# Token arrays split by chunk parity, and each level's transposed factor taken from the evicted factor one level later

## The chip, the core and the metric

One core of a Trainium2 chip runs the whole program. The metric is the device time of one execution in microseconds. The engines are TensorE (PE), VectorE (DVE), ScalarE (ACT), GpSimd (POOL) and SyncE (SP), which issues the DMAs. Each engine works through a queue of its own in program order, and they meet at semaphores.

## What is computed

A two-layer encoder over two sequences of 256 tokens, 1024 features: layer 0 mixes tokens with a bidirectional RWKV-7 recurrence (16 heads of 64), layer 1 with grouped-query attention, and each is followed by a gated MLP. The change lies in the recurrence, once per direction and head:

```python
def step(S, inp):
    r_t, w_t, k_t, v_t, a_t, b_t = inp
    sa = jnp.einsum('bhij,bhj->bhi', S, a_t)
    S = S * w_t[:, :, None, :] + sa[..., None] * b_t[:, :, None, :] + v_t[..., None] * k_t[:, :, None, :]
    return S, jnp.einsum('bhij,bhj->bhi', S, r_t)
y = (_wkv_scan(r4, dec4[0], kd4[0], v4, -kk, kk * a4[0], reverse=False)
     + _wkv_scan(r4, dec4[1], kd4[1], v4, -kk, kk * a4[1], reverse=True))
```

All of it is float32.

## The kernel before

The recurrence is done in chunks of C = 64 tokens. 512 tokens make NCH = 8 chunks, CPS = 4 per sequence; NDIR = 2 directions. The 16 heads are taken as KT = 8 pairs, two heads of 64 features filling the 128 partitions. Inside a chunk the recurrence becomes a triangular 64x64 system, one for each chunk, head and direction, 32 in all for a pair. Its inverse is built by doubling blocks in LEVELS = 5 levels: `mc` holds the factor so far, `mt` its transpose, `nt` the system. A level is a system product (`level_system`, L773/L774) whose result DVE evicts with a mask into `xc` (L1827), then a factor product (`level_factors`, L787/L788) that ACT evicts into `mc` (L1360; in the last level into `mf`, L1363). Levels 0 to 3 have a third product, `xc` by `mt` (L795), which gives the next transpose; ACT evicts direction 0 of it into `mt` (L1366), DVE direction 1 (L1858).

Around the levels stand: `system` (L743), whose result DVE masks into `nt` (L1803, L1805), with the identity added on DVE (L1807, L1809) and on GpSimd (L2044, L2047); `first_factors` (L752, L758, L759); `grams` (L813, 128 columns, and L817), evicted by DVE (L1877, L1881) into `gk` and `gb`; `transposed` (L833), evicted by ACT (L1328) into `kb` and `vt`. The scan over the chunks of a sequence has, for each step j, `from_values` (L841), `from_state` (L851), `solved` (L860, followed at once by key-value products L868, a state copy L870 and the values of the next step), `next_state` (L879), evicted by ACT (L1320) and DVE (L1788, L1793); `outputs` (L891, L897, L903) ends a scan, evicted by L1390. Preparation of a pair (decays, rates, keys, exponentials, scans of decays: L662, L678, L1276, L1297 to L1300, L1721, L1726, L1754 to L1756) and its norm and gate (L722, L727, L733, L1770) fill the rest. Small products of the conditioning (L559, L713) use bank 7.

A software pipeline written out by hand sets the order: `stage(i)` for i from -1 to 8 scans pair i, solves pair i+1, prepares pair i+2 and norms pair i-1. Each engine has its own `stage`, with the same levels in the same order; the loop is unrolled, so the PE program of these stages is straight-line code. Stage -1 solves and prepares alone, stage 6 has no preparation, stages 7 and 8 no solving.

Which part of the 128x128 array a 64x64 matmul uses follows from the partitions of its input (rows) and its output (columns). With `halves` both are the head's half, so two tiles take turns. With `across` direction 1 goes to the other half of the output, and four tiles take turns; L773/L774, L787/L788 and L758/L759 are written that way. Every fp32 matmul shows as two load records and two matmul records.

## Time and profile before

| | us |
|---|---|
| median of three runs | 1939.32 |
| lowest, highest | 1933.93, 1939.99 |
| profiled execution | 1933.49 |
| its span | 1931.7 |
| of it the RWKV stages (251.5 to 752.5) | 501.0 |

The profile is of one execution. Its busy times add up what one engine did; a record of a matmul is longer than the distance to the next, since matmuls overlap, so pace is read from starts and counts. A wait is the idle time of an engine before an instruction, with what released it; "issue" stands for idle time in which it waited for nothing that the profile shows.

### The profile page before, as it was taken

What the parts mean: (1) busy time and instruction counts of PE and PEld (TensorE: products, weight loads), DVE (VectorE), ACT (ScalarE), POOL (GpSimd) and SP (SyncE); (2) the same over time, 40 slices, a digit from 0 to 9 for tenths busy, and PEclk for the clock granted to TensorE, in tenths of its full rate; (3) what the DMA queues carried; (4) which work ended last, traced back from release to release, by engine and by line L of the source; (5) the groups of instructions that cost most, each with busy time, mean ns of one, the idle gap of its engine ahead of it and who ended that gap; (6) DMA issues with size and microseconds to landing.
All of it is one profiled execution on the core that took longest, in us unless ns stands there. A gap on an engine that the chain in (4) does not pass through costs nothing.

```text
span 1931.7 us, 45633 instructions
## 1 busy us (share of the span) xinstructions
PE 1703.5 (88%) x20212; PEld 1339.5 (69%) x20212; DVE 917.4 (47%) x1151; ACT 718.0 (37%) x1118; POOL 588.6 (30%) x298
## 2 busy tenths in 40 slices
PE   4999768999999987879999999967878599999995
PEld 2777257888788885647777888735657388888884
DVE  3755655676666744263333430076662644444103
ACT  3422334444344422353343332243443444444221
POOL 0433032122212200423333444332102334444443
PEclk8999889999999998989999999978988799999997
DMA  7231000111111002435662232201111122333321
GB/s 307 88 128 35 27 7 8 47 53 31 31 51 49 27 5 68 153 145 204 238 240 86 87 120 90 73 11 55 43 45 55 33 87 87 98 96 105 105 75 44
DMA packets 43884, 161.13 MB, mean 83 GB/s; under 512 B 3664, under 2 KB 18256, under 8 KB 40912
## 3 DMA queue, kind: packets, MB, share of 16 engines
q1 hardware_dynamic: 43728, 158.75, 23.8%
q8 instruction: 134, 2.20, 0.4%
q14 instruction: 22, 0.18, 0.0%
HBM read 156.64 MB, written 2.10 MB: 82 GB/s over the span
## 4 chain that ended last, share of the span: by engine, by line
PE 82%; DVE 10%; ACT 4%; issue 3%; POOL 1%; DMA 1%; ACTq 0%; DVEq 0%; SPq 0%; POOLq 0%
PE ps L532 15%; PE ps L533 15%; PE ps L534 14%; PE ps L795 3%; PE ps L633 2%; PE ps L634 2%; PE ps L635 2%; PE ps L559 2%; PE ps L833 2%; DVE x_res L1573 2%; PE ps L787 1%; DVE area L1920 1%; PE ps L813 1%; PE ps L774 1%; DVE area L1503 1%
## 5 line engine op out<-in xcount | busy, mean ns | idle before, releaser
L1998 POOL TENSOR_TENSOR split_w<-raw_w,split_w 128x1024 fp32r<-128x1024 f32 (+1 forms) x148 | 380.7, 2573 | 743.7 <-ACT split_w L1140 743.7
L533 PE MATMUL ps<-h_lo_pad,split_w 128*128 128x512 f32 x800 | 321.3, 402 | 0.0
L532 PE MATMUL ps<-h_hi,split_w 128*128 128x512 f32 x704 | 283.3, 402 | 17.5 <-DVE h_lo_pad L1512 17.4
L1140 ACT ACTIVATE split_w<-raw_w 128x1024 fp32r<-128x1024 f32 (+1 forms) x148 | 167.2, 1130 | 353.9 <-PE ps L534 353.7
L534 PE MATMUL ps<-h_hi,split_w 128*128 128x512 f32 x704 | 279.6, 397 | 0.0
L532 PE MATMUL ps<-ff_hi,split_w 128*128 128x512 f32 x448 | 178.8, 399 | 8.3 <-DVE h_lo_pad L1512 8.3
L532 PEld LDWEIGHTS ps<-h_hi,split_w 128*128 128x128 f32 x704 | 133.8, 190 | 68.8 <-issue 29.1
L534 PE MATMUL ps<-ff_hi,split_w 128*128 128x512 f32 x448 | 175.8, 392 | 0.0
L533 PEld LDWEIGHTS ps<-h_lo_pad,split_w 128*128 128x128 f32 x800 | 152.0, 190 | 33.7 <-issue 0.5
L1587 DVE SCALAR_TENSOR_TENSOR ffs<-ffs,fcur 128x512 f32<-128x512 f32 x44 | 82.6, 1876 | 176.5 <-ACT ffs L1173 176.5
L1552 DVE TENSOR_TENSOR sx<-sx,ffs 128x512 f32<-128x512 f32 x32 | 22.2, 693 | 290.0 <-ACT ffs L1108 290.0
L534 PEld LDWEIGHTS ps<-h_hi,split_w 128*128 128x128 f32 x704 | 133.1, 189 | 31.8
L533 PE MATMUL ps<-ff_lo,split_w 128*128 128x512 f32 x352 | 136.9, 389 | 0.0
L532 PEld LDWEIGHTS ps<-ff_hi,split_w 128*128 128x128 f32 x448 | 84.8, 189 | 30.4 <-issue 9.2
L534 PEld LDWEIGHTS ps<-ff_hi,split_w 128*128 128x128 f32 x448 | 84.8, 189 | 18.3
L2037 POOL TENSOR_TENSOR split_p<-o_res,split_p 128x1024 fp32r<-128x1024 f32 x24 | 57.9, 2412 | 128.9 <-ACT split_p L1251 128.9
L633 PE MATMUL ps<-x_split,split_p 128*128 128x512 f32 x192 | 78.0, 406 | 18.5 <-DVE x_split L1647 10.1
L1595 DVE TENSOR_TENSOR ffs<-ffs,ps 128x512 f32<-128x512 f32 x44 | 30.3, 688 | 123.6 <-ACT ffs L1177 123.6
L1108 ACT ACTIVATE ffs<-ps 128x512 f32<-128x512 f32 x32 | 19.1, 598 | 166.1 <-PE ps L534 166.1
L634 PE MATMUL ps<-x_split,split_p 128*128 128x512 f32 x192 | 77.5, 404 | 0.0
L635 PE MATMUL ps<-x_split,split_p 128*128 128x512 f32 x192 | 77.3, 402 | 0.0
L533 PEld LDWEIGHTS ps<-ff_lo,split_w 128*128 128x128 f32 x352 | 66.1, 188 | 13.5
(267 smaller groups left out, 3361.4 us busy)
## 6 DMA issues: line engine op xcount, KB each, us to landing
raw_w<-in_ffn_up SPq DMA_DIRECT2D x88, 512.0 KB, 3.6
raw_w<-in_ffn_down SPq DMA_DIRECT2D x32, 704.0 KB, 4.1
late_a<-in_ada_w SPq DMA_DIRECT2D x7, 2048.0 KB, 8.4
late_b<-in_ada_w SPq DMA_DIRECT2D x7, 2048.0 KB, 10.1
o_res<-in_proj_w SPq DMA_DIRECT2D x24, 512.0 KB, 3.5
area<-in_ada_w SPq DMA_DIRECT2D x12, 1024.0 KB, 6.1
area<-in_ada_w SPq DMA_DIRECT2D x4, 2048.0 KB, 21.5
x_res<-in_xT SPq DMA_DIRECT2D x2, 2048.0 KB, 11.5
```

The costliest lines, as they stand in the source:

```text
L532: mm(bank, wh[:, o:o + P], hi[:, t], start=(t == 0), stop=False)
L533: mm(bank, wh[:, o:o + P], lo[:, t], start=False, stop=False)
L534: last = mm(bank, wl[:, o:o + P], hi[:, t], start=False, stop=(t == total - 1))
L559: last = mm(bank[g:g + CG, :], csil[:, k, :], blk[:, k, :], start=(k < NCG), stop=(k >= KT - NCG))
L633: mm(ps[:, m, :], wh[:, o:o + P], xh, start=(k == 0), stop=False)
L634: mm(ps[:, m, :], wh[:, o:o + P], xl, start=False, stop=False)
L635: last = mm(ps[:, m, :], wl[:, o:o + P], xh, start=False, stop=(k == KT - 1))
L795: last = mm(ps[lo:hi, 2 + n, c * C:(c + 1) * C], xc[lo:hi, n, c, :], mt[lo:hi, n, c, :], start=True, stop=True)
L1140: A(split_w[:, r % 2, 0, 0:cols], raw_w[:, r, 0:cols], ACT.Copy).then_inc(w_hi, 1)
L1587: own(V.scalar_tensor_tensor(seqs(conv[s]), u_pad[s][:, :, 0:SEQ], fcur[:, s, 0:1], seqs(conv[s]), ALU.mult, ALU.add))
L1998: G.tensor_tensor(split_w[:, r % 2, 1, 0:cols], raw_w[:, r, 0:cols], split_w[:, r % 2, 0, 0:cols].bitcast(F32), ALU.subtract).then_inc(w_l ...
L2037: G.tensor_tensor(split_p[:, n % 2, 1], raw_p[:, n % NRAW, :], split_p[:, n % 2, 0].bitcast(F32), ALU.subtract).then_inc(proj_lo, 1)
```

## The change

The arrays whose partitions are tokens (`nt`, `mc`, `xc`, `mt`, `gk`, `gb`, `kb`, `vt`, `ut`, `x0s`) had the head as the half of the partitions and the chunk as a slot in the free dimension. Now the half is the parity of the chunk, and the slot is the chunk pair with the head. The arrays whose partitions are features stay by head. So a product from features to tokens reads rows by head and writes columns by parity, a product from tokens to features the reverse, and products inside the token space keep one half. The PSUM bank of a token result is chosen by the head, that of a feature result by the chunk's parity or the direction.

The third product of levels 0 to 3 is gone. In levels 1 to 4 `level_transposes` multiplies the evicted `mc` by the identity, right behind the level's system product, and ACT evicts both directions. The order of other work shifts with it: `solved` gives its trailing products to a new `carried`, which waits for the solution (`u_ev`), and `next_state` takes over the key-value products; the lora products move from bank 1 to bank 6; the decay products move behind level 2's factors, the gate behind level 3's; the modulation half stands inside `outputs`; `transposed` is done in three groups, of which the values wait for the gram evictions.

```diff
@@ system @@
-                for n in range(NDIR):
-                    for c in range(NCH):
-                        for lo, hi in halves:
-                            last = mm(ps[lo:hi, 2 + n, c * C:(c + 1) * C], arn[q % 2][lo:hi, n, c, 0:C],
-                                      kbn[q % 2][lo:hi, n, c, C:P], start=True, stop=True)
-                    last.then_inc(sys, 1)
+                for n, c, h in tiles_:
+                    last = mm(ps[rows(c), 2 + h, cell(n, c)], arn[q % 2][head(h), n, c, 0:C], kbn[q % 2][head(h), n, c, C:P],
+                              start=True, stop=True)
+                last.then_inc(sys, 1)
@@ level_factors @@
-                if l < LEVELS - 1:
-                    for n in range(NDIR):
-                        for c in range(NCH):
-                            for lo, hi in halves:
-                                last = mm(ps[lo:hi, 2 + n, c * C:(c + 1) * C], xc[lo:hi, n, c, :], mt[lo:hi, n, c, :],
-                                          start=True, stop=True)
-                        last.then_inc(tmm[n], 1)
+
+            def level_transposes(q, l):
+
+                for c in range(NCH):
+                    o = slice(c * C, (c + 1) * C)
+                    for lo, hi, a, b in across:
+                        one = mm(ps[lo:hi, 2, o], mc[lo:hi, 0, c, :], ident[lo:hi, lo:hi], start=True, stop=True)
+                        two = mm(ps[a:b, 3, o], mc[lo:hi, 1, c, :], ident[lo:hi, lo:hi], start=True, stop=True)
+                one.then_inc(tmm[0], 1)
+                two.then_inc(tmm[1], 1)
@@ the scan on PE @@
+            def carried(p, j):
+
+                pe.wait_ge(u_ev, CPS * p + j + 1)
+                last = from_values(p, j + 1)
+                if j > 0:
+                    for n in range(NDIR):
+                        for q in range(NSEQ):
+                            for h in range(2):
+                                last = mm(ps[head(h), n, s_col(q)], ident[head(h), head(h)], states[head(h), j, n, q, :],
+                                          start=False, stop=False, skip_group_check=True)
+                last.then_inc(carry_mm, 1)
+
+            def next_state(p, j):
+
+                pe.wait_ge(carry_mm, (CPS - 1) * p + j + 1)
+                for f in range(2):
+                    for q, n, h in lanes:
                         c = chunk(n, q, j)
...
+                        right = ut[rows(c), j, h, q, :] if f else vt[rows(c), slot(c, h), :]
+                        last = mm(ps[head(h), n, s_col(q)], kb[rows(c), n, f, slot(c, h), :], right, start=False, stop=(f == 1),
                                   skip_group_check=True)
                 last.then_inc(s_mm, 1)
@@ the order of a stage on PE @@
                     if solves:
                         level_system(q, l)
+                        if l > 0:
+                            level_transposes(q, l)
...
                     elif l == 2:
                         if scans:
                             from_state(p, 2)
-                        if prepares:
-                            lora_decays(r)
...
                         if scans:
-                            if prepares:
-                                pe.wait_ge(evac, 4 * r + 3)
                             solved(p, 2)
+                        if prepares:
+                            lora_decays(r)
...
                 if scans:
-                    outputs(p)
-                if ada_:
-                    modulation_half(2 * p)
+                    outputs(p, first_half)
@@ the order of a stage on ACT @@
+                    if solves and l > 0:
+                        for n in range(NDIR):
+                            act.wait_ge(tmm[n], (LEVELS - 1) * q + l)
+                            A(mt[:, n, :, :], chunks(ps[:, 2 + n, :]), ACT.Copy).then_inc(tev[n], 1)
                     if l == 2 and scans:
                         right_sides(p, 2)
-                    if l == 2 and prepares:
-                        decays(r)
...
-                        if l < LEVELS - 1:
-                            act.wait_ge(tmm[0], (LEVELS - 1) * q + l + 1)
-                            A(mt[:, 0, :, :], chunks(ps[:, 2, :]), ACT.Copy).then_inc(tev[0], 1)
...
                     elif l == 2:
                         if prepares:
+                            decays(r)
                             load_function(ACT.Exp)
@@ the order of a stage on DVE @@
-                    dve.wait_ge(sys, 2 * q + 1)
-                    V.tensor_tensor(nt[:, 0], chunks(ps[:, 2, :]), eight(ct[:, K_NT:K_NT + C]), ALU.mult).then_inc(sys_in, 1)
...
+                    dve.wait_ge(sys, q + 1)
...
+                    dve.wait_ge(sys_in, q + 1)
...
-                    if solves and l < LEVELS - 1:
-                        dve.wait_ge(tmm[1], (LEVELS - 1) * q + l + 1)
-                        V.tensor_copy(mt[:, 1, :, :], chunks(ps[:, 3, :])).then_inc(tev[1], 1)
```

## Rows read from the trace of the kernel before

**Rows 1.** The page: the span, and PE's busy time, share and instructions.
```profile
span 1931.7 us, 45633 instructions
PE 1703.5 (88%) x20212; PEld 1339.5 (69%) x20212; DVE 917.4 (47%) x1151; ACT 718.0 (37%) x1118; POOL 588.6 (30%) x298
```

**Rows 2.** The stretches of the stages: length, busy (records) by engine, clock, DMA.
```profile
core 0: us, PE busy (x) PEld busy (x) DVE busy (x) ACT busy (x) POOL busy (x), PEclk, DMA share, GB/s
251.50:305.43 53.93, 43.33 (x1360) 37.12 (x1360) 31.74 (x49) 21.78 (x37) 13.34 (x10) 0.92 0.03 7
305.44:363.72 58.28, 54.95 (x1874) 49.07 (x1874) 33.24 (x54) 24.16 (x44) 13.67 (x10) 1.00 0.08 25
363.73:669.02 305.29, 291.19 (x9424) 252.68 (x9420) 202.76 (x300) 129.15 (x240) 66.98 (x50) 1.00 0.14 42
669.03:726.90 57.87, 51.73 (x1854) 48.30 (x1850) 26.62 (x38) 15.50 (x30) 2.87 (x2) 1.00 0.02 5
727.00:752.50 25.50, 20.05 (x473) 16.54 (x470) 9.13 (x13) 3.44 (x8) 0.00 (x0) 0.93 0.14 46
```

**Rows 3.** PE in order of time: start, duration, line, operation, tiles, count [idle before].
```profile
422.80 2.08 PE L743 MATMUL ps<-area 64*64 64x64 f32 x64
...
424.72 0.63 PE L841 MATMUL ps<-area 64*64 64x64 f32 x16
...
432.69 1.45 PE L678 MATMUL ps<-area 64*128 64x256 f32 x4
...
474.36 3.71 PE L813 MATMUL ps<-area 64*64 64x128 f32 x64
```

**Rows 4.** A stretch of PE within one run of L773/L774.
```profile
438.55:439.48 0.93, 0.93 (x63) 1.00 0.00 0
```

**Rows 5.** PE's weight loads after a pause that waited for nothing, in a row.
```profile
684.87 0.13 PEld L773 LDWEIGHTS ps<-area 64*64 64x64 f32 x1 [0.54 <-issue]
...
688.36 0.13 PEld L788 LDWEIGHTS ps<-area 64*64 64x64 f32 x1 [0.60 <-issue]
...
691.84 0.13 PEld L774 LDWEIGHTS ps<-area 64*64 64x64 f32 x1 [0.36 <-issue]
```

**Rows 6.** The two stretches between these three pauses, columns as in rows 2.
```profile
684.87:688.35 3.48, 3.02 (x127) 2.88 (x127) 3.11 (x4) 0.00 (x0) 0.00 (x0) 1.00 0.02 5
688.36:691.83 3.47, 3.26 (x127) 3.12 (x128) 2.78 (x3) 1.57 (x3) 0.00 (x0) 1.00 0.02 5
```

**Rows 7.** The page's queue of instruction fetches: pieces, MB, share.
```profile
q8 instruction: 134, 2.20, 0.4%
```

**Rows 8.** DVE in order of time: gram evictions, masked evictions, decay scan.
```profile
298.61 2.47 DVE L1877 TENSOR_TENSOR area<-ps,ct 128x512 f32<-128x512 f32 x4
...
432.36 1.29 DVE L1827 TENSOR_TENSOR area<-ps,ct 128x512 f32<-128x512 f32 x2 [1.46 <-PE ps L773]
...
452.95 2.30 DVE L1721 TENSOR_TENSOR_SCAN area<-ct,area 128x512 f32<-128x512 f32 x1
...
475.50 0.69 DVE L1877 TENSOR_TENSOR area<-ps,ct 128x512 f32<-128x512 f32 x1 [0.75 <-PE ps L813]
```

**Rows 9.** ACT in order of time, in the first level of a full stage.
```profile
435.29 1.08 ACT L1360 ACTIVATE area<-ps 128x512 f32<-128x512 f32 x2 [3.35 <-PE ps L787]
...
436.88 1.28 ACT L1315 ACT_TABLE_LOAD   x1
...
438.28 0.36 ACT L1320 ACTIVATE area<-ps 128x256 f32<-128x256 f32 x1
438.73 1.26 ACT L1276 ACTIVATE h_pad<-ps,pcur 128x512 f32<-128x512 f32 x2
```

**Rows 10.** GpSimd in order of time, at the head of the stage of 422.80.
```profile
424.77 1.27 POOL L2044 TENSOR_TENSOR area<-area,ct 128x512 f32<-128x512 f32 x1 [12.81 <-DVE area L1803]
426.11 1.60 POOL L2047 TENSOR_TENSOR area<-area,ct 128x512 f32<-128x512 f32 x1
```

**Rows 11.** A stretch of DVE, from level 4's masked eviction to the last product.
```profile
463.18:474.75 11.57, 9.61 (x16) 1.00 0.02 4
```

**Rows 12.** A stretch of PE: L743 of the first stage.
```profile
251.52:255.15 3.63, 3.63 (x65) 0.50 0.02 5
```

249 lines of the change are left out of this document (141 added, 108 removed).

## The prediction, made before the changed kernel was run

> **What bounds the kernel now.** I read the page first, then the stretches, then single runs of one engine. The page gives a span of 1931.7 us with PE busy for 88% [rows 1]. The change touches only the pipelined RWKV part, so the next view is that part cut at the starts of L743, the first product of each stage [rows 2]: a first stage of 53.9 us that only solves, one of 58.3, five full ones of 305.29 together (61.1 each), one of 57.9 without preparation, and a tail of 25.5 with scans alone. In the five full ones PE is busy for 95% (291.2 of 305.3) and DVE for 66%, so a full stage ends when PE has worked through its queue. What PE does there is run 64x64 matmuls, each of which shows as two records. The reader is to see their pace, not their durations (an fp32 record shows some 0.22 us, but records overlap). L743, whose heads lie in array tiles (0,0) and (1,1), starts 64 records in 1.92 us, up to L841: 30 ns a record. L813, the same two tiles but 128 columns, needs 3.55 us for 64: 55 ns [rows 3]. L773/L774 alternate over all four tiles and put 63 records into 0.93 us: 15 ns [rows 4].
>
> A second limit lies just beneath. PE's weight loads show pauses that wait for nothing: at 684.87, 688.36 and 691.84 [rows 5]. Between these lie 127 matmuls and 127 loads, then 127 and 128, that is one block of 256 instructions (a start on the edge falls out), in 3.48 and 3.47 us [rows 6]. The page's instruction queue moved 2.20 MB in 134 pieces, 16.4 kB each or 256 instructions of 64 bytes [rows 7]. So I read: a new block of 256 PE instructions can't begin sooner than 3.47 us after the one before. A full stage has (9424 + 9420)/5 = 3769 instructions, 14.7 blocks, so no less than 51.1 us, however fast the matmuls are. In sentences that the sum can do without: the Trainium skill (Runtime: NRT & Kernel Launch, Instruction fetch mechanics) says that PE's instruction memory holds 2048 instructions and that fetching is hidden behind issue. The pauses above speak against "hidden" for 15 ns matmuls; by that rule this floor would be absent, and the stage would come to the 52.6 us worked out below.
>
> **The change part by part.**
> Tiles. System, grams, transposes, state and output products now use input rows by head and output rows by chunk parity (or the reverse), so four tiles alternate. Of the full stage's records this is L743 64, the former third product's place 256, L817 64, L833 160, L897 and L903 128, L851, L868 and L879 48 each: 816 that go from 30 to 15 ns, 12.2 us, and L813's 64 from 55 to some 28, 1.8 us. Together 14.0 us of PE pace. L841, L860, L870 and L891 stay on two tiles. The number of instructions is unchanged: 64 transposing records for levels 1 to 4 stand where the 64 of the third product for levels 0 to 3 stood. With pace alone the stage would be 61.1 - 14.0 = 47.1, under the floor of 51.1, so the full 14 us can't come back.
>
> Transposed factor. It was made right after the factor from the same operands, L795 x64 in 1.9 us, and evicted half by ACT, half by DVE. Now it is made from the evicted factor after the level's system product, and ACT evicts both halves, in order after everything ACT had queued in the level before. Its path per level is: system 0.94, transposes 0.94, 0.25 to the eviction (the first quarter of L813, 0.89 us from 474.36, is evicted from 475.50 [rows 3, 8]), 1.08 for two evictions [rows 9], 0.1, factors 0.94, 0.25, 1.08, 0.1: 5.7 us. DVE's two masked evictions (1.29 [rows 8]) run beside the transposes and ACT's pair, and cost nothing as long as DVE comes to them in time.
>
> I lay a full stage out with these durations, from the stage's L743.
> Head, to the level-0 system: now 431.1 - 422.8 = 8.3 (DVE's first masked eviction starts at 432.36, 1.2 behind the product [rows 3, 8]). L743 shrinks by 1 us, but both parities must be there before the eviction, which then takes 1.3 for both, and only then GpSimd starts its two steps, of 1.27 and 1.60 us [rows 10]. They end 5.4 after L743's start, where they ended at 4.9; PE then waits, having less to do. Unchanged: 8.35 us.
> Level 0: no transposes, but the key scales with their 1.45 us [rows 3] lie between system and factors: 5.9.
> Level 1: ACT leaves level 0's factors at 5.6 after the system's start, then loads a table (1.28 and a short 0.2), takes the right sides (0.4) and the rates (1.26) [rows 9], to 8.75. The transposes are ready at 7.85 and wait for ACT until 8.75; factors at 9.95, next system at 12.5. That is 6.6 by waits, but the level has 544 instructions, 2.1 blocks, 7.4 us: the floor decides.
> Level 2: 5.9. The decay products move behind its factors, so DVE's scan (2.30 [rows 8]), which was early, now waits for ACT's decays until 19.8 and ends at 22.1. Behind it stands level 3's masked eviction, and behind that PE's factors.
> Level 3: so factors start only at 23.5, next system at 25.9: 7.5 where the level's own path would be 5.7. This is the added wait that I see. From level 0's system to level 4's: 25.9 by waits, 26.4 by the floor (1948 instructions); neither fills the other's holes fully, so I take 27.2.
> Tail, from level 4's system to the next L743. DVE's work decides: 1.2 to its start, then what it now does in 463.18 to 474.75, 9.6 us busy [rows 11], then four gram evictions of 2.47 together [rows 8], two more, 1.3; after that PE's transposes 0.95, ACT's two evictions 1.45, 0.15. With small waits 18.3. The 1420 instructions there need 19.2 by the floor, and outputs no longer cover anything. I take 19.4.
> Sum: 8.35 + 27.2 + 19.4 = 55.0 against 61.1: 6.1 less. By waits alone, with no floor: 8.35 + 25.9 + 18.3 = 52.6.
>
> All stages: five full ones -30.5. The one of 58.3, without norms but with scans, -5 (the same levels; its PE was busy for 94%). The one of 57.9, without preparation, has 3704 instructions, floor 50.2, and no ACT tables in its way: 52.7, -5. The first, of 53.9, has no scans: its pace never bound, L817/L833 and the grams save about 3 at its end, level 3 loses 1, DVE's gram evictions set its end: -3. The last, 25.5: states now wait for the solution before the value products (0.5 + 0.5 + 0.5 over steps, partly under L1770), outputs save 1.9: 0, between -1 and +2. Sum -43.5. What the laying out forgets (semaphore steps, pauses that fall on the path) I set at 0.5 a stage, +4. So -39.5: 1933.5 (the profiled run: span 1931.7 and 1.8 around it) becomes 1894. The median of the runs shown, 1939.3, stands 5.8 above the profiled run, and the forecast is for a median: 1900.
>
> Unknown prices. Four tiles with same-column neighbours: no row shows this order (L773/L774 alternate otherwise, though over the same four tiles). Bounds: 15 ns as there, 30 ns as L743. I take 15, since the new order also comes back to a tile only after the three others, and also keeps each half of the input rows on its own PSUM bank. 128 columns on four tiles: 28 to 55 ns, taken at 28; the rest would be 1.8 us a stage. Strided evictions (heads interleaved): between no cost and 0.3 us each by the spread of L1827 and the slower pair work of DVE; I take none. A gain there is excluded, the sizes being equal.
>
> **Rivals.**
> A. The floor isn't there (pauses belong to something else, or are absorbed). Then 52.6 a full stage, -8.5 each, about -58 in all: 1881. For it: PE has only these three pauses in a row in the rows. Against: their distance is equal to 0.01 us.
> B. Evictions and their order bind harder: ACT now evicts both transposed halves, and each level waits behind side work in two engines. If level 1 and level 2 too lose 2 us as level 3 does, the stage is 58.5 to 59, and the sum -18: 1921. For it: DVE is busy for 66% and its queue is in program order. Beside it: the Trainium skill (TensorEngine Tiling (Array Packing), PSUM Bottleneck) says that after tiling the copies out of PSUM may become the bound; by rows 2 ACT is busy for 42%, so I hold it for a matter of order, not of load.
> C. The other side: slower. PE, no longer full, loses its granted clock. Rows show both levels: L743 at 0.50 (1.2 GHz) takes 3.6 us [rows 12] against 1.9 at full clock, after a stretch in which PE had waited. All full stages are at 1.00 now. At half clock a full stage's PE pace would be twice 47.1, 94 us, so +33 a stage instead of -6; the gain is eaten once about 15% of the stages' time is at half clock (39.5 of 39 x 7). At a quarter of it: 1900 + 0.25 x 39 x 7 = 1968. Against: the first stage waits more than I expect of later ones (PE busy 80%) and still has 0.92.
> D. The change doesn't do what it says: same-column tiles don't overlap, pace stays at 30 ns. Then the stage is as now, plus or minus 1: 1935 to 1945.
>
> **How the numbers follow.** The forecast's case 0.46, A 0.22, B 0.19, C 0.06, D 0.07. The range is to reach over A and B: low 1874 (A with 1 us a stage more), high 1927 (B and a piece of C). About 0.3%, or 6 us, is what a measurement here tells from no change. Faster: forecast, A, B: 0.87. Same: D 0.06. Slower: C and the rest of D, 0.07.
>
> **What would show it.** Right: in the stretches, full stages of 55 us with PE instructions at 3769 and pauses every 256 of them at 3.5 us in most blocks; L743 at 15 ns a record; PE waiting for ACT's transposed eviction in level 1 and for DVE in level 3; DVE nearly gapless from level 4's eviction to the last gram. Wrong: blocks of 256 under 3.2 us (A); factors that wait for ACT in every level (B); granted clock under 0.95 in full stages (C); L743 still at 1.9 us (D). A first stage that gains more than 6 us would mean that the third product stood on its path.

## The result, and the profile after

The changed kernel is slower: 1956.93 us, the median of four runs (1954.61 to 1958.76), against 1938.92 for the kernel before beside it. The ratio is 1.0103, 95% interval 1.0086 to 1.0120. The forecast was 1900, with 1874 to 1927 around it, and gave slower a chance of 0.07.

| us | before | after | forecast |
|---|---|---|---|
| profiled execution | 1933.5 | 1954.6 | 1894 |
| first stage | 53.9 | 56.7 | 51 |
| second stage | 58.3 | 65.5 | 53 |
| five full stages, each | 61.1 | 62.2 | 55.0 |
| stage without preparation | 57.9 | 64.3 | 53 |
| last stage | 25.5 | 28.8 | 25.5 |

The head of the page, and the stretches of the stages as in [rows 2] (length, busy time and records by engine, granted clock, DMA):

```profile
span 1952.8 us, 45651 instructions
PE 1640.3 (84%) x20212; PEld 1259.3 (64%) x20212; DVE 894.9 (46%) x1119; ACT 733.7 (38%) x1150; POOL 595.1 (30%) x298
...
q8 instruction: 134, 2.20, 0.5%
...
PE 75%; DVE 10%; ACT 6%; issue 5%; POOL 2%; DMA 1%; ACTq 0%; DVEq 0%; SPq 0%; POOLq 0%
```

```profile
core 0: us, PE busy (x) PEld busy (x) DVE busy (x) ACT busy (x) POOL busy (x), PEclk, DMA share, GB/s
252.05:308.73 56.68, 37.10 (x1360) 30.45 (x1360) 29.11 (x45) 23.61 (x41) 13.42 (x10) 0.85 0.03 7
308.74:374.20 65.46, 50.15 (x1874) 42.13 (x1874) 31.46 (x50) 26.14 (x49) 14.22 (x10) 0.87 0.08 23
374.21:685.07 310.86, 249.79 (x9420) 200.41 (x9420) 187.28 (x280) 138.86 (x261) 71.53 (x50) 0.95 0.14 41
685.08:749.40 64.32, 45.56 (x1850) 39.34 (x1850) 23.64 (x34) 17.41 (x34) 3.36 (x2) 0.92 0.02 5
749.41:778.24 28.83, 20.89 (x473) 15.33 (x470) 9.16 (x13) 3.49 (x8) 0.00 (x0) 0.76 0.13 40
```

The count of instructions is the same and PE is busy for 63 us less in the span, 41 of them in the five full stages (291.2 to 249.8), so the tiles do what was expected. None of it shows in the lengths. PE was busy for 95% of a full stage and is now for 80%, and the granted clock, 1.00 in all five before, is 0.95. It fell from 1.00 to 0.87 in the second stage and to 0.92 in the one without preparation, and from 0.93 to 0.76 in the last. These three lose 17 us together, the five full ones 5.6, the first one 2.8: 25 us in the stages, from 501.0 to 526.2. The two profiled spans differ by 21, since the parts ahead of the stages and behind them took 4 us less in this execution; no run tells a cause for that.

The pace is as forecast. The solution and value products of the outputs (L933, L938), on four tiles in the new order, run at 14 to 15 ns a record (two stretches of PE; in the second, the grams):

```profile
487.34:489.22 1.88, 1.88 (x132) 1.88 (x132) 1.88 (x2) 1.85 (x3) 1.88 (x2) 1.00 0.21 31
489.25:493.67 4.42, 3.19 (x141) 2.71 (x132) 4.42 (x10) 0.99 (x3) 0.80 (x1) 1.00 0.74 230
```

The second stretch shows where such a gain goes. The grams' 64 records of 128 columns and 64 of 64 columns would take 2.8 us at the paces of 28 and 15 ns, and take 4.42: in them lie a pause without a cause and a wait for DVE's eviction (weight loads in order of time):

```profile
489.20 1.39 PEld L829 LDWEIGHTS ps<-area 64*64 64x64 f32 x49
491.22 0.42 PEld L829 LDWEIGHTS ps<-area 64*64 64x64 f32 x15 [0.63 <-issue]
492.73 1.02 PEld L835 LDWEIGHTS ps<-area 64*64 64x64 f32 x64 [1.09 <-DVE area L1928]
```

The groups of waits of the weight loads over the five full stages (us in total, times, longest) show both kinds. In the kernel before, the same view begins with waits for nothing (L787 13.4, L773 6.4); its first wait for an engine is 2.3.

```profile
PEld ps L804 <- ACT area L1401: 15.1, 13, 1.8
PEld ps L769 <- POOL area L2099: 12.9, 5, 2.6
PEld ps L790 <- ACT area L1408: 10.0, 13, 0.8
PEld ps L790 <- issue: 8.0, 9, 1.5
PEld ps L835 <- issue: 5.2, 3, 3.1
PEld ps L814 <- issue: 4.8, 6, 1.9
```

To add this up I split each full stage by the starts of PE's weight loads: time in which PE works, idle time ahead of a load that has a semaphore to wait for, and idle time ahead of one that has none (at the edges of blocks of 256 instructions for the greater part); matmuls of over 0.35 us and gaps under 0.06 us count as work. A pause that falls on an instruction with a semaphore is so counted as a wait, and the views above, which go by what released PE, can call such a wait "issue". Mean of the five full stages, in us; the last column is the time at half clock (1.2 GHz), which lies inside the others.

| kernel | stage | works | waits for an engine | waits for nothing | at half clock |
|---|---|---|---|---|---|
| before | 61.1 | 56.8 | 0.9 | 3.4 | 0.0 |
| after | 62.2 | 47.2 | 7.9 | 7.1 | 6.1 |
| run 1: layout alone | 64.1 | 50.9 | 8.8 | 4.4 | 7.5 |
| run 2: transposes alone | 62.4 | 53.9 | 3.0 | 5.6 | 0.7 |
| run 7: direction cut, order as before | 61.8 | 47.2 | 6.6 | 8.0 | 6.1 |
| run 9: after + small products in the head | 64.2 | 48.7 | 5.7 | 9.7 | 5.5 |
| run 10: after + wide products in the head | 61.2 | 47.4 | 5.0 | 8.8 | 2.7 |
| run 11: after, 48 output products fewer | 59.9 | 46.6 | 9.3 | 4.1 | 9.1 |
| run 12: after + direction cut + wide products | 62.1 | 48.7 | 4.2 | 9.3 | 6.1 |
| run 17: after, wide for small in the outputs | 59.2 | 45.5 | 7.4 | 6.3 | 2.7 |
| run 18: run 12, wide for small in the outputs | 59.7 | 46.9 | 4.7 | 8.1 | 2.0 |

PE works 9.6 us less, waits 7.0 more for others and 3.7 more for nothing. The sum is +1.1 instead of -6.1.

The head of a full stage, as GpSimd and PE show it (the stage from 435.53):

```profile
435.53 1.53 PE L760 MATMUL ps<-area 64*64 64x64 f32 x63
...
437.16 1.29 DVE L1853 TENSOR_TENSOR area<-ps,ct 128x512 f32<-128x512 f32 x2 [4.06 <-PE ps L760]
...
438.48 0.69 DVE L1861 TENSOR_TENSOR area<-area,ct 128x512 f32<-128x512 f32 x1
...
438.53 1.77 POOL L2096 TENSOR_TENSOR area<-area,ct 128x512 f32<-128x512 f32 x1 [10.71 <-DVE area L1853]
...
440.37 1.59 POOL L2099 TENSOR_TENSOR area<-area,ct 128x512 f32<-128x512 f32 x1
...
442.02 0.97 PE L769 MATMUL ps<-ct,area 64*64 64x64 f32 x26 [2.42 <-POOL area L2099]
```

GpSimd's two steps end 6.4 us after the first product, where they ended at 4.9 [rows 3, 10]; the forecast was 5.4. Its first step takes 1.77 us where it took 1.27; it now starts 0.05 us behind DVE's addition of the identity, where it used to start ahead of it. PE stands for 2.4 us, and 1.4 us later runs at half clock, with most of the first factors and the start of level 0's system in it (a stretch of PE):

```profile
443.40:446.80 3.40, 3.40 (x57) 1.78 (x51) 0.69 (x1) 1.36 (x4) 0.00 (x0) 0.50 0.02 5
```

Such a stretch of 3.4 us begins 6.5 to 7.9 us into four of the five full stages, 14 of their 31 us at half clock. The other 17 lie elsewhere, 14 of them 45 us or more into a stage.

### The profile page after: what moved, and what is told of

Its sections match the earlier page's. It is cut to its first block, busy times and chain, and to the rows that moved or that the text cites. A ratio compares the mean times of both kernels' runs of the same rounds, so it can differ in the third digit from the quotient of the medians.

```text
span 1952.8 us, 45651 instructions
## 1 busy us (share of the span) xinstructions
PE 1640.3 (84%) x20212; PEld 1259.3 (64%) x20212; DVE 894.9 (46%) x1119; ACT 733.7 (38%) x1150; POOL 595.1 (30%) x298
## 4 chain that ended last, share of the span: by engine, by line
PE 75%; DVE 10%; ACT 6%; issue 5%; POOL 2%; DMA 1%; ACTq 0%; DVEq 0%; SPq 0%; POOLq 0%
PE ps L538 15%; PE ps L539 15%; PE ps L540 14%; PE ps L639 2%; PE ps L640 2%; PE ps L641 2%; PE ps L565 2%; DVE x_res L1621 2%; PE ps L804 2%; DVE area L1551 1%; PE ps L790 1%; DVE area L1972 1%; PE ps L654 1%; PE ps L805 1%; PE ps L1081 1%
## 5 line engine op out<-in xcount | busy, mean ns | idle before, releaser
L1600 DVE TENSOR_TENSOR sx<-sx,ffs 128x512 f32<-128x512 f32 x32 | 22.2, 692 | 289.4 <-ACT ffs L1148 289.4
L2089 POOL TENSOR_TENSOR split_p<-o_res,split_p 128x1024 fp32r<-128x1024 f32 x24 | 57.9, 2414 | 129.4 <-ACT split_p L1291 129.4
L1148 ACT ACTIVATE ffs<-ps 128x512 f32<-128x512 f32 x32 | 19.2, 599 | 165.5 <-PE ps L540 165.5
L1881 DVE TENSOR_TENSOR area<-ps,ct 128x512 f32<-128x512 f32 x80 | 51.3, 683 | 61.3 <-PE ps L790 61.3
```

Of the source, the lines that this page charges most:

```text
L1881: V.tensor_tensor(xc[:, n, :, :], chunks(ps[:, 4 + n, :]), msk, ALU.mult).then_inc(xev[n], 1)
L2089: G.tensor_tensor(split_p[:, n % 2, 1], raw_p[:, n % NRAW, :], split_p[:, n % 2, 0].bitcast(F32), ALU.subtract).then_inc(proj_lo, 1)
```

## The experiments

Ratios are to the kernel before, measured beside each kernel; I compare kernels by their ratios, at 19.4 us for 1%. The kernels named "fill" add products whose results nobody reads and leave the output as it is; the eleventh, the seventeenth and the eighteenth leave terms of the output out, and the third adds work ahead of the stages.

| run | kernel | median us | ratio (95%) |
|---|---|---|---|
| 1 | layout alone | 1969.5 | 1.0169 (1.0132 to 1.0206) |
| 2 | transposes alone | 1945.7 | 1.0030 (1.0015 to 1.0046) |
| 4 | half of the transposes evicted by DVE | 1960.1 | 1.0120 (1.0083 to 1.0157) |
| 5 | after + fill | 1939.0 | 1.0034 (1.0018 to 1.0050) |
| 6 | after, order as before | 1962.0 | 1.0147 (1.0126 to 1.0168) |
| 7 | 6 + direction cut | 1943.0 | 1.0044 (1.0020 to 1.0068) |
| 8 | 7 + fill | 1936.4 | 1.0009 (0.9995 to 1.0022) |
| 9 | after + 64 small products in the head | 1958.9 | 1.0137 (1.0098 to 1.0177) |
| 10 | after + 2 wide products in the head | 1940.3 | 1.0033 (1.0019 to 1.0046) |
| 11 | after, 48 output products fewer | 1924.5 | 0.9939 (0.9916 to 0.9963) |
| 12 | after + direction cut + fill | 1936.3 | 1.0004 (0.9984 to 1.0023) |
| 13 | 12 + merged transposes | 1941.0 | 1.0011 (0.9997 to 1.0025) |
| 14 | 1 + direction cut + fill | 1942.9 | 1.0008 (0.9987 to 1.0029) |
| 15 | before + fill in the last scan | 1941.7 | 1.0007 (0.9991 to 1.0023) |
| 16 | after + merged transposes | 1954.9 | 1.0071 (1.0041 to 1.0102) |
| 17 | after, 48 small products for 4 wide | 1929.7 | 0.9948 (0.9930 to 0.9965) |
| 18 | 12, 48 small products for 4 wide | 1922.2 | 0.9911 (0.9893 to 0.9929) |

### The two parts apart (1, 2)

The layout alone takes the changed kernel and puts the third product back behind the factors, with its evictions by ACT and DVE; the transposes alone take the kernel before and replace the third product.

```diff
+                if l < LEVELS - 1:
+                    for n in range(NDIR):
+                        for c in range(NCH):
+                            for lo, hi in halves:
+                                last = mm(ps[lo:hi, 2 + n, c * C:(c + 1) * C], xc[lo:hi, n, c, :], mt[lo:hi, n, c, :],
+                                          start=True, stop=True)
...
-                        if l > 0:
-                            level_transposes(q, l)
```

> The changed kernel with the third product of levels 0 to 3 put back (two tiles, evicted half by ScalarE, half by VectorE), everything else as changed. Theory P (the late transpose stands on each level's dependent path and costs more than the four tiles bring): the layout alone is faster than the kernel before, full stages of 56 to 58 us, 1900 to 1920 us. Theory F (fetch pauses and granted clock eat what PE saves, wherever the saving comes from): full stages of 59 to 62 us, 1930 to 1955 us.

> The kernel before with the third product taken out and the transposes of the evicted factor one level later in its place, both directions evicted by ScalarE; layout and order else as before. Theory P: slower than before, since every level from 1 on gets 0.94 for the transposes, 0.25 and 1.1 us for the evictions ahead of its factors, partly under the system's own eviction: 1.5 to 3 us a stage, 1950 to 1965 us. Theory F: PE has 3.7 us a stage less to do, fetch and clock eat it: 1930 to 1945 us.

Measured: the layout costs 1.7% (33 us), more than either theory gave it, the transposes alone 0.3% (6 us), and on top of the layout the transposes give 13 us back (1.0169 to 1.0103). So the loss sits in the layout, the part that saves most of the pace. In the table of full stages the layout alone takes PE's work from 56.8 to 50.9 and the waits for other engines from 0.9 to 8.8. Of these 4.8 stand ahead of the factors: in each level from 1 on PE waits 0.7 to 1.8 us for DVE's masked eviction, and goes on 0.12 us after its end in 19 of 20 cases. In the changed kernel the transposes stand in that place.

### The pace and the blocks by themselves (3)

The kernel before, with runs of unused 64x64 products on PE that wait for nothing: 512 products on four tiles written out, the same 512 as a loop of 16 times 32, then 256 on two tiles, 256 in the order of the new layout, and 256 of these with 128 columns.

```diff
+            micro(ACROSS4, C, 512)
+            with pe.Fori(0, 16):
+                micro(ACROSS4, C, 32)
+            micro(HALVES2, C, 256).then_inc(micro_sem, 1)
...
+            micro(PARITY4, C, 256)
```

> The kernel before with runs of PE matmuls without any wait ahead of the first stage: 512 64x64 matmuls over four tiles in straight-line code, 512 of the same in a loop of 32 each, 256 over two tiles, 256 over four tiles in parity order, 256 of these with 128 columns. If blocks of 256 PE instructions can't come faster than 3.47 us: the straight four-tile run takes 8 blocks, 28 us, at 27 ns a record, the looped one 15 ns a record, 15 us; two tiles 30 ns in either case; parity order 27 ns; 128 columns 28 ns. If fetching is hidden: straight and looped runs both take 15 us.

Stretches: two blocks of the written-out run, the loop, two tiles, the new order, a block with 128 columns. Then the weight loads of the written-out run:

```profile
233.42:237.41 3.99, 2.09 (x128) 1.96 (x128) 0.00 (x0) 0.00 (x0) 0.00 (x0) 1.00 0.02 4
249.43:253.42 3.99, 2.09 (x128) 1.96 (x128) 0.00 (x0) 0.00 (x0) 0.00 (x0) 1.00 0.01 4
257.87:275.36 17.49, 17.49 (x1036) 16.29 (x1031) 0.00 (x0) 0.00 (x0) 0.00 (x0) 1.00 0.00 1
275.41:290.33 14.92, 14.92 (x525) 14.92 (x516) 0.00 (x0) 0.00 (x0) 0.00 (x0) 1.00 0.02 4
290.60:302.88 12.28, 8.18 (x511) 7.77 (x515) 0.00 (x0) 0.00 (x0) 0.00 (x0) 1.00 0.02 5
304.65:308.65 4.00, 3.72 (x128) 3.48 (x128) 0.00 (x0) 0.00 (x0) 0.00 (x0) 1.00 0.01 4
```

```profile
245.43 1.95 PEld L998 LDWEIGHTS ps<-ct 64*64 64x64 f32 x128 [0.51 <-issue]
249.43 1.96 PEld L998 LDWEIGHTS ps<-ct 64*64 64x64 f32 x128 [2.05 <-issue]
253.44 1.95 PEld L998 LDWEIGHTS ps<-ct 64*64 64x64 f32 x128 [2.05 <-issue]
```

The same products take 29.5 us written out and 17.5 in a loop. Written out, PE runs 256 instructions in 2 us and stands for 2; the blocks began 4.00 us apart, the last one 3.73. In the loop there are no pauses and the pace is 17 ns a record. Two tiles need 29 ns, or 3.7 us for 256 instructions, and show no pauses. So the floor is there, since only the sending of new instructions differs between the written-out run and the loop. Its size isn't one number: this run, which asks without a break, got 4.00, but the one in the new order asked without a break too, and its blocks came 3.4 to 3.7 us apart; with 128 columns it was 3.9 to 4.0, at 29 ns a record. What sets it between these no run shows. In the full stages of after, pauses a block apart (those over 0.06 us) lie 3.3 to 4.0 us from each other in 29 of 37 cases, and 4.1 to 6.7 in the rest.

The sentence of the Trainium skill that the forecast weighed (Runtime: NRT & Kernel Launch, Instruction fetch mechanics: crossing a block is mostly hidden) holds here for two tiles, without a pause in 14.9 us, and not for four, which stand for half of the time.

### Who evicts, and the order of the side work (4, 6)

Run 4: DVE evicts direction 1 of the transposes. Run 6: decays and gate stand where they stood before.

```diff
@@ 4 @@
+                        if l > 0:
+                            dve.wait_ge(tmm[1], (LEVELS - 1) * q + l)
+                            V.tensor_copy(mt[:, 1, :, :], chunks(ps[:, 3, :])).then_inc(tev[1], 1)
@@ 6 @@
                     elif l == 2:
                         if scans:
                             from_state(p, 2)
+                        if prepares:
+                            lora_decays(r)
```

> The changed kernel, but VectorE evicts direction 1 of the level transposes, right after its two masked evictions, and ScalarE direction 0 alone. If ScalarE's queue holds the factors up (theory Q): PE's waits for these evictions, 17 to 22 us in the stages, fall by half or more, 1940 to 1948 us. If the path is long whoever evicts (P), or fetch and clock decide (F): 1950 to 1960 us.

> The changed kernel with the decay products (PE ahead of level 2's factors, ScalarE ahead of level 2's eviction) and the gate (ahead of level 3's factors) back at the places of before. Theory O (the moved steps hold level 3 up: its masked eviction stands behind the decay scan): level 2 to 3 shorter by 1 to 2 us a stage, 1945 to 1951 us. If the waits are set by the level's path alone: 1953 to 1960 us.

Neither is the cause. The split changes nothing that the interval shows (1.0120 against 1.0103), PE's waits for other engines stay at about 8 us a full stage, and the order of before costs 0.4% more. What the forecast feared of the moved decays does stand in the trace (the scan waits 1.99 us for ACT, and the masked eviction of level 3 behind it), and is still the better order here; with cut and fill the two orders are level (8 and 12):

```profile
469.15 1.48 DVE L1769 TENSOR_TENSOR_SCAN area<-ct,area 128x512 f32<-128x512 f32 x1 [1.99 <-ACT area L1316]
470.55 1.25 DVE L1881 TENSOR_TENSOR area<-ps,ct 128x512 f32<-128x512 f32 x2
```

### The clock (5, 15)

Fill: a 128x512 and a 128x256 product ahead of the first factors, where PE waits for GpSimd, and 128x256 ones ahead of the waits of the last scan. Run 15 puts the latter alone into the kernel before.

```diff
                 if solves:
+                    filler(4, TOK)
+                    filler(5, TOK // 2)
                     first_factors(q)
```

> The changed kernel with wide products of constants added in PE's waits: 128x512 and 128x256 ahead of first_factors in every stage (into banks 4 and 5, which are free there), 128x256 ahead of each wait of the last scan. Nothing reads them. Theory C (granted clock): the time at half clock from the first stage to the output projection, 103 us in the changed kernel against 23 before, falls below 60 us, and the kernel gets faster by 8 to 15 us, 1942 to 1949 us, though work was added. If the clock doesn't matter (W, the waits alone): 1957 to 1965 us.

> The kernel before with three wide unused products (128x256) ahead of the waits of the last scan, and nothing else. The clock is at its lower level there in the kernel before as well. If holding the clock up is worth time in the tail by itself, 3 to 6 us less than before (1933 to 1936); if those products only stand in the way, 0 to 2 us more.

Five's stretches of the second, the last but one and the last stage, to be read beside those of after:

```profile
307.11:366.04 58.93, 45.77 (x1878) 37.34 (x1878) 31.58 (x50) 26.01 (x49) 14.20 (x10) 1.00 0.08 25
679.03:738.78 59.75, 45.30 (x1854) 38.98 (x1854) 23.65 (x34) 17.29 (x34) 3.37 (x2) 0.94 0.02 5
738.79:763.89 25.10, 22.61 (x492) 15.45 (x490) 9.21 (x13) 3.49 (x8) 0.00 (x0) 0.94 0.14 47
```

Work added makes the kernel 0.7% faster (13 us). Time at half clock in the pipeline (from the first stage to the output projection) falls from 103 of 540 us to 50 of 524; the second stage goes from 65.5 to 58.9 at a clock of 1.00 for 0.87, the one without preparation from 64.3 to 59.8, the last from 28.8 to 25.1. The full stages gain nothing (62.6), though none of their stretches at half clock begins in the first 20 us any more. So the third rival was real, in the stages at the two ends more than in the full ones. In the kernel before the three products of the last scan are worth nothing (1.0007); the head's were not tried there.

### The head of the stage (7, 8, 12, 14)

DVE's two masked evictions are cut by direction instead of by head, so that GpSimd can start after the first.

```diff
-                    for h in range(2):
-                        last = V.tensor_tensor(nt_h[:, :, :, h, :], ps[:, 2 + h, :].rearrange("p (n c s) -> p n c s", n=NDIR, c=PAIRS),
-                                               both, ALU.mult)
...
+                    for n in range(NDIR):
+                        last = V.tensor_tensor(nt_h[:, n].rearrange("p c h s -> p h c s"),
+                                               ps[:, 2:4, n * PAIRS * C:(n + 1) * PAIRS * C].rearrange("p h (c s) -> p h c s", c=PAIRS),
+                                               one_way, ALU.mult)
+                        last.then_inc(sys_in, 1)
...
-                pool.wait_ge(sys_in, q + 1)
+                pool.wait_ge(sys_in, 2 * q + 1)
```

> e6_order_back, and the system's two masked evictions cut by direction across both banks, where the changed kernel cuts by head, so that GpSimd starts after the first. The head of the stage (first product to level 0) falls from 10.6 to 9.9 us if this start is what it hangs on: 4 to 6 us less than e6_order_back; else the same.

> e7_direction_first with the fillers of e5_fillers. If order, head and clock are separate costs, their gains add: 1930 to 1940 us, level with the kernel before. If they are the same waits counted thrice: 1945 to 1952 us.

> The changed kernel with the cut by direction in the head and the fillers, the order as changed (e8_together had the order put back, which cost 8 us beside the changed kernel). If the three effects add: 1957 - 12 (fillers) - 12 to 19 (direction) = 1926 to 1933 us, level with the kernel before or a little faster. If fetching holds the floor: 1933 to 1940 us, as e8_together.

> The new layout alone (third product kept; 1969.5 us as it stood) with the head mended (masked evictions cut by direction) and the clock held up (wide unused products in the head's wait and in the last scan's). If head and clock were all that the layout lost, what is left is its saved pace, and it beats the kernel before: 1900 to 1925. If the fetch of PE's instructions takes what the pace saves, it ends level with the kernel before or above: 1937 to 1950.

GpSimd's first two steps in run 6, and in run 7, which differs by the cut alone (there with DVE's addition above them):

```profile
369.24 1.77 POOL L2097 TENSOR_TENSOR area<-area,ct 128x512 f32<-128x512 f32 x1 [10.93 <-DVE area L1854]
371.09 1.59 POOL L2100 TENSOR_TENSOR area<-area,ct 128x512 f32<-128x512 f32 x1
```

```profile
371.85 1.26 DVE L1862 TENSOR_TENSOR area<-area,ct 128x512 f32<-128x512 f32 x1
...
371.29 1.27 POOL L2097 TENSOR_TENSOR area<-area,ct 128x512 f32<-128x512 f32 x1 [12.00 <-DVE area L1856]
372.64 1.59 POOL L2100 TENSOR_TENSOR area<-area,ct 128x512 f32<-128x512 f32 x1
```

The cut is worth 1.0% (20 us) from 6 to 7, where 4 to 6 were expected: the head goes from 10.5 to 8.9 us, and the step is back at 1.27, since it starts ahead of DVE's addition again. That addition then takes 1.26 us where it took 0.69. Each of the two steps is the longer one when it starts while the other runs. In the order of before, cut and fill nearly add: 27 us from 6 to 8, where 20 and 13 were measured apart. In the order of the changed kernel they give 19 us (12), 6 more than the fill alone; the cut alone wasn't run there. Both close the same wait, so some overlap is likely, but its size isn't shown. With both, the changed kernel is level with the one before, and so is the layout alone (14: 31 us back from 1.0169). Here the upper branch of 14's expectation held: head and clock mended, the saved pace is still worth nothing.

### How many instructions (9, 10, 11, 13, 16, 17, 18)

9 and 10 put unused work into the wait of the head: 64 small products on four tiles (256 PE instructions, 1.9 us) or two wide ones (8 instructions, 1.5 us). 11 leaves out the value products and half of the solution products of the outputs, 192 instructions and 1.4 us of pace. 17 and 18 leave the same out and put four unused 128x212 products in their place, 16 instructions and 1.4 us.

```diff
@@ 10 (9: 64 products of 64x64 in its place) @@
+                for bank, cols in ((4, TOK), (5, 3 * P)):
+                    mm(ps[:, bank, 0:cols], ident, ct[:, K_RES:K_RES + cols], start=True, stop=True)
@@ 17, 18 (11: without the two added lines) @@
-                for n, c, h in tiles_:
-                    mm(ps[head(h), c % 2, cell(0, c)], vt[rows(c), slot(c, h), :], gk[rows(c), n, slot(c, h), C:P],
-                       start=False, stop=False, skip_group_check=True)
-                for j in range(CPS):
+                for k in range(4):
+                    mm(ps[:, k % 2, 0:212], ident, ct[:, K_RES:K_RES + 212], start=False, stop=False, skip_group_check=True)
+                for j in range(2, CPS):
@@ 13, 16 @@
-                        for h in range(2):
-                            last = mm(ps[rows(c), (2, 4)[n] + h, cell(f, c)], kbn[q % 2][head(h), n, c, f * C:(f + 1) * C],
-                                      ident[head(h), head(h)], start=True, stop=True)
+                        last = mm(ps[rows(c), (2, 4)[n] + f, c // 2 * P:(c // 2 + 1) * P], kbn[q % 2][:, n, c, f * C:(f + 1) * C],
+                                  ident, start=True, stop=True)
```

> The changed kernel with 64 small products over four tiles (256 PE instructions, 1.9 us of pace) ahead of first_factors in every solving stage, where PE waits 2.6 us; nothing reads them. Theory F (a block of 256 PE instructions costs 3.5 to 4 us whatever its pace): the block can't be hid in the wait and every full stage gets 1.5 to 4 us longer, less what the clock gives back: slower than e10_fill_wide by 12 us or more. If the count of instructions doesn't matter: equal to e10_fill_wide within 4 us.

> The same place and the same PE time, 1.9 us, but as two wide products (8 PE instructions). Theory C: half-clock time falls, 4 to 10 us less than the changed kernel, 1947 to 1953 us. Without an effect of the clock: 1957 us. Both theories of e9_fill_small put it below that one (F) or level with it.

> The changed kernel without the value products and without half of the solution products of outputs, so its outputs lack these terms: 96 records, 192 PE instructions and 1.4 us of pace less in each of 8 scans. Theory F: 0.75 of a block at 3.5 to 4.0 us, 21 to 24 us less than the changed kernel, 1933 to 1936 us. By pace alone: at most 11.5 us less, 1945 us; if VectorE's products and gram evictions set the end of the stage, as forecast: 0 to 3 us less.

> The kernel of the twelfth run (the changed kernel with its masked evictions cut by direction and wide unused products in the head's wait and in the last scan's; 1936.3 us) with fewer and larger products for the same data: the transposes of token arrays and values go two heads at a time, 128 rows by 64 columns against the whole identity (16 products instead of 32 for each direction, 8 instead of 16 for the values), and the carried state is copied by 4 products instead of 8. 44 products less, about 176 PE instructions of a stage, at about the same PE time, since a product on two tiles takes 30 ns a record where one on four takes 15. Fetch theory (what paces a full stage is how many instructions PE is sent, 3.5 to 4.0 us for 256): 176/256 x 3.5 to 4.0 x 8 stages = 19 to 22 us less, 1914 to 1918. Waits theory (a full stage is set by PE's waits for evictions, and instructions beside them are free): 1930 to 1937.

> The changed kernel with the merged products alone (44 products, about 176 PE instructions, less in a stage at about the same PE time). Fetch theory: 19 to 22 us less than the changed kernel's 1957, 1935 to 1938. Waits theory: 1950 to 1957. If the clock decides (less PE work means more time at half clock), 1957 or over.

> The changed kernel with the same 48 small products of outputs left out as in the eleventh run (the value products and half of the solution products; their terms are missing from the output), but the PE time put back in the same place: four unused products of 128x212, 16 PE instructions for 192, with 4 x 0.35 = 1.4 us of PE time for 48 x 30 ns = 1.4. Since the merged transposes turned out to take more PE time than those they replaced (128 columns, not 64), this is the clean form of that question. Fetch theory (the number of PE instructions sets the tail): most of the eleventh run's gain stays, 176/256 x 3.5 to 4.0 x 8 = 19 to 22 us less than the changed kernel, 1935 to 1938. Pace theory (the eleventh run gained by PE time and by ending sooner): 1950 to 1957, as the changed kernel.

> The same exchange (48 small products of outputs for four wide ones of equal PE time, the terms missing from the output) on the kernel of the twelfth run, whose head and clock are mended (1936.3 us). Fetch theory: 19 to 22 us less, 1914 to 1918. Waits theory (with head and clock mended the evictions set the stage): 1932 to 1937.

The merged transposes (13, 16, with the carried states copied by half as many products) stayed outside what the fetch theory expected: 1941.0 for 1914 to 1918, and 1954.9 for 1935 to 1938. They tell nothing apart, since their expectation was wrong: a product of two heads has 128 columns, not 64. The transposes of one direction are 64 records from 483.53 in after, and 32 from 479.19 in run 16, longer with half the instructions:

```profile
483.53 1.48 PE L850 MATMUL ps<-ct,area 64*64 64x64 f32 x64
```

```profile
479.19 1.97 PE L849 MATMUL ps<-ct,area 128*64 128x128 f32 x32
```

PE's work went up by 1.3 to 2.1 us a stage, which can have eaten what the count saved.

The exchanges at about equal PE time tell more. The five full stages of run 9, of run 10, and of runs 12 and 18, in this order:

```profile
368.97:689.89 320.92, 258.69 (x10060) 209.92 (x10060) 187.83 (x280) 139.03 (x260) 70.32 (x50) 0.96 0.14 40
```

```profile
366.71:672.64 305.93, 250.20 (x9440) 199.29 (x9440) 188.65 (x280) 138.60 (x261) 70.33 (x50) 0.98 0.14 42
```

```profile
362.69:673.33 310.64, 256.89 (x9440) 204.91 (x9440) 185.07 (x280) 138.14 (x261) 67.80 (x50) 0.95 0.14 41
```

```profile
364.47:662.84 298.37, 249.80 (x9000) 197.67 (x9000) 186.29 (x280) 138.39 (x260) 68.38 (x50) 0.98 0.14 43
```

In the head 248 instructions more (and 0.4 us of PE time) cost 20 us over eight stages, 2.5 a stage, although they fill a wait. The traces show where: the head of a full stage takes 11.9 us in 9 and 9.3 in 10, the rest of the stage 52.3 and 51.9, and PE's waits for nothing in the head are 2.4 and 0.1 us. In the second full stage of 9 such a pause stands in the middle of the fill:

```profile
439.03 1.20 PE L769 MATMUL ps<-ct 64*64 64x64 f32 x66 [3.13 <-issue]
```

In the outputs 176 fewer at the same PE time give 30 us (17) of the 32 that leaving them out altogether gives (11), and 18 us on the mended kernel (18), 2.3 a stage, where 19 to 22 was expected of the fetch and 0 to 4 of the waits. DVE's, ACT's and GpSimd's work is the same between 12 and 18 and between 9 and 10.

17 and 18 don't separate fetch and clock, since the time at half clock falls as well. From the first stage to the output projection it goes from 103 to 70 us in 17, and from 50 to 38 between 12 and 18; PE's waits for nothing fall by 11 and 5 us, its work by 14 and 7. Run 11 does separate them, since it puts nothing in: the time at half clock stays (103 and 107 us), PE's work falls by 12 us, about the pace left out, the waits for nothing fall by 27, and the waits for other engines grow by 9. Both 11 and 17 got 8 us or more beyond what was expected of the fetch, and that surplus stays open.

## Why the prediction was wrong

The reading of the bound was right: PE's pace bound the kernel before, and a floor of blocks lay under it. The sum then failed for the full stage, 62.2 us instead of 55.0: the head came out 2.2 too long, the levels 1.6, the part behind them 3.5. The step that failed is the one by which floor and waits all but cover each other (27.2 from 26.4 and 25.9, 19.4 from 19.2 and 18.3). The sum had 7.9 us for both on top of a pace of 47.1; PE's work took 47.2, and waits for engines and pauses for nothing took 7.9 and 7.1, one after the other. The clock, weighed as a rival alone, stood in the sum at nothing.

**Pace (-14.0 a stage).** Right in kind: 15 ns a record on four tiles, 28 for 128 columns without the pauses. PE's work fell by 9.6 us; of the rest 2.5 to 3 are the 5 to 6 us that it spent at half clock, which would have been half as long, and 1.5 to 2 stay open. That PE's work came out at the forecast's 47.1 is in part luck, since the forecast took the 14.0 from a whole stage of 61.1, of which only 56.8 was work. The strided evictions cost nothing, as forecast: two masked ones take 1.29 us, four of the grams 2.47, as before [rows 8].

**The floor (3.47 us a block).** I took the distance of three pauses in a kernel that rarely asked for more, and treated it as a rate. Asked without a break, a block takes 3.4 to 4.0 us (run 3), so 14.7 blocks take 50 to 59 us, not 51.1; which rate holds in a stage isn't shown. Worse, I took little more than the longer of floor and waits, part by part. The part behind level 4's system shows it best: 18.3 by waits, 19.2 by the floor, 19.4 forecast, 22.9 measured, as the sum of 17.4 of work, 4.1 of pauses and 1.4 of waits for engines. At 4.00 us a block its 1420 instructions would need 22.2; two of the five ran in 20.8 and 20.9, both without any half clock, and the other three, with 3.4 to 6.7 us of it, in 22.8 to 26.4. So floor and clock both stand in this term. The kernel before lay closer to the floor than I saw: two tiles need 3.7 us for 256 instructions (run 3), so its pace and the fetch were nearly in balance, and the saved pace had little to give from the start. Runs 9 and 10 show that in the head the stage follows the count, and run 11 that fewer instructions take pauses away at the same clock. That the time between blocks is the fetch of instructions is my reading of the loop, which has no pauses; its mechanism wasn't seen.

**The head ("unchanged, 8.35").** 10.6 measured. (The 8.35 was that of three of the five full stages; their mean before was 8.9.) The step put GpSimd's end at 5.4 us after the first product; it was 6.4. One of the pauses (0.25) fell into the first product, and GpSimd's first step grew by 0.5 us beside DVE's addition, which I hadn't priced, having placed the two next to each other. Worse was what I wrote next: that PE then waits "having less to do", at no cost. Half clock followed that wait in four of the five full stages, and no longer does so with the fill (5, 10, 12), where it comes later in the stage instead. The head cost 20 us in all (6 to 7), 13 of it by its own length (1.6 a stage), the rest by what followed from it.

**The levels (27.2).** 28.8. Level 0 was 5.9 as forecast, level 1 7.2 (7.4), level 3 7.9 (7.5), with the waits that were named: ACT's transposed eviction behind the rates in level 1, DVE's scan behind the decays in level 3. Level 2 took 7.7 instead of 5.9. There the floor and the waits don't take turns, as I had it, but add: a pause of 1.6 us fell ahead of the last of the transposes, so that ACT's second eviction came 1.2 us late, and the factors behind it (ACT, and PE's last matmul of the transposes, in level 2):

```profile
462.41 0.60 ACT L1401 ACTIVATE area<-ps 128x512 f32<-128x512 f32 x1 [3.42 <-PE ps L814]
464.23 0.60 ACT L1401 ACTIVATE area<-ps 128x512 f32<-128x512 f32 x1 [1.22 <-PE ps L815]
```

```profile
463.98 0.21 PE L815 MATMUL ps<-ct,area 64*64 64x64 f32 x1 [1.61 <-issue]
```

**The other stages (-3, -5, -5, 0).** They became +2.8, +7.2, +6.4 and +3.3, at a clock of 0.85, 0.87, 0.92 and 0.76. Unused products alone bring 1.3, 6.5, 4.6 and 3.7 of these back (5). The first rival (no floor) is out by run 3. The second (evictions bind) named the 7.0 us of waits, but moving an eviction or the order brought nothing (4, 6). The third, slower by the clock, had the right sign and a chance of 0.06; its bar (the gain is eaten at 15% of the stages' time at half clock) took the whole forecast gain as there to be eaten, while the other terms had left none of it. 103 of 540 us, 19%, were at half clock, and taking half of that away gave 13 us. The fourth (tiles don't overlap) is out by the pace. What made the sign come out wrong is that the floor, the head and the clock were weighed as cases apart, though they stand in the same stage together.

No kernel with the full output beat the kernel before; the best of them is level with it (12).

## What to carry to other kernels

A faster matmul is worth only what the next limit leaves, and in straight-line PE code of small matmuls the number of instructions can be that limit: measure the time of a block with a run that waits for nothing before counting on pace, and prefer one wide product to many small ones as long as its columns don't cost more PE time. When PE is made faster, price the waits that it will then have at both clock levels. Where one engine's start moves behind all of another's pieces, cut the pieces so that the first releases it, and look at what then runs beside it.

## What the runs showed of the hardware

- Written-out 64x64 fp32 matmuls on four tiles: 15 ns a record inside a block of 256 instructions, then a pause up to 4.00 us from the block's start; in the tile order of the new layout up to 3.4 to 3.7. The same matmuls in a loop: 17 ns a record with no pause.
- The 64 small products of run 9 cost 2.5 us a stage more than run 10's two wide ones, in a place where PE had been waiting 2.4 us anyway, and the pauses for nothing in the head grew from 0.1 to 2.4 us: instructions that fill a wait are not free.
- A GpSimd addition of two 128x512 inputs takes 1.77 us when it starts just behind a DVE addition from SBUF (run 6). It takes 1.27 when it starts during a DVE eviction from PSUM, even though a DVE addition begins halfway through it; then that one takes 1.26 us instead of 0.69 (run 7). The Trainium skill (GPSIMD Engine Reference, Specifications) says that GpSimd shares its SBUF interfaces with VectorE and contends with VectorE instructions of two SBUF inputs; the rows of runs 6 and 7 agree, and show that the one that starts second pays.
